# An attention loop one stage shorter, with its causal mask added by TensorE

## What is computed

```python
s_cmp = einsum(q, kc) * scale;  p_cmp = masked_softmax(s_cmp, ends <= t);  o_cmp = p_cmp @ vc
s     = einsum(q, ks) * scale;  p     = masked_softmax(s, kpos <= tq);     o_s   = p @ vs
s     = einsum(q, kw) * scale;  p     = masked_softmax(s, mw);             o_w   = p @ vw
o = g[..., 0:1] * o_cmp + g[..., 1:2] * o_s + g[..., 2:3] * o_w
```

## Time and profile before

| | |
|---|---|
| median of 3 executions | 2720.64 us (2716.98 to 2725.18) |
| the profiled execution | 2725.98 us |
| its span | 2724.3 us |
| busy share TensorE / VectorE / ScalarE | 98% / 68% / 51% |
| attention loop | about 1702 to 1826 us of the span |
| mean granted TensorE clock, whole span | 0.981 |

### The profile page before, as it was taken

The page is one execution under the profiler, slowest core; times in us unless marked ns, Lnnn a source line. Parts: engine busy times, 40 slices in busy tenths (PEclk is TensorE's granted clock), DMA queues, the critical chain, the costliest instruction groups (busy, mean ns, idle before and its releaser), DMA issues.

```text
span 2724.3 us, 42687 instructions
## 1 busy us (share of the span) xinstructions
PE 2658.9 (98%) x16032; PEld 2340.0 (86%) x16032; DVE 1855.1 (68%) x2662; ACT 1400.2 (51%) x1882; POOL 147.9 (5%) x149
## 2 busy tenths in 40 slices
PE   7999999999999999999999999889999999999998
PEld 7999898888888888888888888678888888888887
DVE  4699866677766775677755767756677757765775
ACT  5588755356634553454444544643456535543553
POOL 0001100210000000003100000002200000000003
PEclk9999999999999999999998999789999999999999
DMA  6454335555555555555755665005555555555544
GB/s 210 160 180 146 109 122 168 183 192 185 187 194 190 185 186 192 192 178 174 212 157 171 185 189 171 9 14 185 189 185 188 191 192 186 185 189 193 188 162 147
DMA packets 238535, 464.49 MB, mean 170 GB/s; under 512 B 12506, under 2 KB 14170, under 8 KB 238426
## 3 DMA queue, kind: packets, MB, share of 16 engines
q1 hardware_dynamic: 236922, 460.73, 51.0%
q10 hardware_dynamic: 1504, 2.29, 0.3%
HBM read 460.90 MB, written 2.10 MB: 170 GB/s over the span
## 4 chain that ended last, share of the span: by engine, by line
PE 88%; DVE 4%; DMA 4%; ACT 3%; issue 1%; SPq 0%; DVEq 0%; ACTq 0%
PE bank L1723 47%; PE bank L1726 23%; PE bank L1969 4%; PE bank L1970 4%; PE bank L1971 4%; DVE weight_tail L1083 1%; ACT weight_head L605 1%; PE bank L2005 1%; DMA weight_raw<-in_ffn_w_up 1%; PE bank L2047 1%; DMA w<-in_nsa_cmp_w 1%; DMA weight_raw<-in_cd_w_in 1%; DMA weight_raw<-in_ffn_w_down 1%; ACT prob L1047 1%; PE bank L2084 1%
## 5 line engine op out<-in xcount | busy, mean ns | idle before, releaser
L1083 DVE TENSOR_TENSOR weight_tail<-weight_raw,weight_head 128x2048 fp32r<-128x2048 f32 (+1 forms) x456 | 1000.5, 2195 | 757.2 <-ACT weight_head L605 755.6
L605 ACT ACTIVATE weight_head<-weight_raw 128x2048 fp32r<-128x2048 f32 (+1 forms) x456 | 832.3, 1826 | 969.0 <-DMA weight_raw<-in_ffn_w_up 315.9
L1723 PE MATMUL bank<-norm_in,weight_head 128*128 128x512 f32 x3840 | 1210.8, 397 | 11.4 <-DVE residual L1439 6.7
L1726 PEld LDWEIGHTS bank<-norm_in,weight_tail 128*128 128x128 f32 x3840 | 723.4, 188 | 171.4
L1726 PE MATMUL bank<-norm_in,weight_tail 128*128 128x256 f32 x3840 | 755.9, 278 | 0.0
L1723 PE MATMUL bank<-mixed,weight_head 128*128 128x512 f32 x2176 | 703.6, 398 | 6.7 <-DVE mixed L1500 3.6
L1723 PEld LDWEIGHTS bank<-norm_in,weight_head 128*128 128x128 f32 x3840 | 586.5, 189 | 13.2 <-DVE weight_tail L1083 7.5
L1726 PEld LDWEIGHTS bank<-mixed,weight_tail 128*128 128x128 f32 x2176 | 411.5, 189 | 80.8
L1726 PE MATMUL bank<-mixed,weight_tail 128*128 128x256 f32 x2176 | 463.6, 280 | 0.0
L1723 PEld LDWEIGHTS bank<-mixed,weight_head 128*128 128x128 f32 x2176 | 348.5, 190 | 26.8 <-DVE residual L1439 5.2
L1969 PE MATMUL bank<-norm_in,weight_head 128*128 128x256 f32 x896 | 260.8, 291 | 6.7 <-ACT zx L855 4.4
(11 more groups left out here) (288 smaller groups left out, 1583.1 us busy)
## 6 DMA issues: line engine op xcount, KB each, us to landing
weight_raw<-in_ffn_w_up SPq DMA_DIRECT2D x176, 1024.0 KB, 4.9
weight_raw<-in_ffn_w_down SPq DMA_DIRECT2D x64, 1024.0 KB, 5.0
weight_raw<-in_cd_w_in SPq DMA_DIRECT2D x64, 1024.0 KB, 5.7
weight_raw<-in_ab_w_in SPq DMA_DIRECT2D x56, 1024.0 KB, 4.9
weight_raw<-in_ab_w_out SPq DMA_DIRECT2D x32, 768.0 KB, 4.3
weight_raw<-in_ffn_w_down SPq DMA_DIRECT2D x32, 768.0 KB, 4.2
weight_raw<-in_cd_w_out SPq DMA_DIRECT2D x32, 768.0 KB, 4.2
x_stage<-in_x SPq DMA_DIRECT2D x4, 512.0 KB, 6.0
```

The source lines that it names most:

```text
L605: act.activation(WHEAD[:, off % RING, 0:kt * CW], WRAW[:, off % RING, 0:kt * CW], ACT.Copy)\
L1083: dve.tensor_tensor(WTAIL[:, off % RING, 0:kt * CW], WRAW[:, off % RING, 0:kt * CW], WHEAD[:, off % RING, 0:kt * CW].bitcast(F32), ALU.sub ...
L1723: pe.matmul(bank[c][:, :], head, rhs[:, u * s.kt + k, :], start=u == 0 and k == 0, stop=False)
L1726: mm = pe.matmul(bank[c][:, 0:SEQ], tail, rhs[:, u * s.kt + k, 0:SEQ], start=False, stop=u == s.units - 1 and k == s.kt - 1)
```

## The change

Transposes, value products and the copies that belong to them come one iteration sooner on every engine: TensorE transposes item n - 2 and multiplies item n - 3 in iteration n, ScalarE copies item n - 2, and the output copies of a head (1052 and 1685) stand at even n from 6 on in place of odd n from 7 on. PROB has 3 buffers and another place. Each engine's loop runs one iteration less.

The causal mask is no longer added by VectorE. GpSimd writes a mask of one 128x128 block and a copy of the identity, both in the rounded type fp32r. TensorE accumulates identity times mask onto the last 128 columns of both branches, right behind the scores. VectorE takes the maxima straight from PSUM, and ScalarE reads the scores from PSUM in its exponentials; only the compressed scores still pass through PROB. So the scores of item n now also wait for the exponentials of item n - 2 (p_ready), and for the transposed copy of item n - 3 in place of n - 4. The diff, cut:

```diff
-PROBS = 4
-        MASK = at("causal", places["tri"], [P, 2 * P], F32)
+        IDENT_R = at("ident_r", places["tri"], [P, P], F32R)
+        MASK_R = at("causal", places["ust"], [P, P], F32R)
-        PROB = at("prob", places["norm_in"] + 22528, [P, PROBS, 528], F32)
+        PROB = at("prob", places["norm_in"] + 8192, [P, 3, 528], F32)
...
-            link(pool.memset(MASK[:, :], 0.0))
-            pool.affine_select(out=MASK[:, P:2 * P], in_=MASK[:, P:2 * P], compare_op=ALU.is_ge, fill=NEG,
+            pool.tensor_copy(IDENT_R[:, :], IDENT[:, :]).then_inc(mask_ready, 1)
+            link(pool.memset(MASK_R[:, :].bitcast(F32), 0.0))
+            pool.affine_select(out=MASK_R[:, :], in_=MASK_R[:, :].bitcast(F32), compare_op=ALU.is_ge, fill=NEG,
                                base=0, pattern=[[-1, P]], channel_multiplier=1).then_inc(mask_ready, 1)
...
-            for n in range(last + 6):
+            for n in range(last + 5):
-                if 3 <= n < last + 3:
-                    m = n - 3
+                if 2 <= n < last + 2:
+                    m = n - 2
...
-                    act.activation(PTC[0:NCMP, m % 2, :], bank[2 + m % 2][0:NCMP, P:2 * P], ACT.Copy).then_inc(pt_read, 1)
+                    act.activation(PTC[0:NCMP, m % 2, :], bank[3 - m % 2][0:NCMP, P:2 * P], ACT.Copy).then_inc(pt_read, 1)
...
-                    for r, probs in enumerate((PROB[:, p3, 512:512 + NCMP], PROB[:, p3, 0:nk], PROB[:, p3, SEQ:SEQ + nk])):
-                        act.activation(probs, probs, ACT.Exp, bias=MX[:, 4 * b + r:4 * b + r + 1], scale=SCALE,
+                    if n >= 3:
+                        act.wait_ge(pt_done, n - 2)
+                    branches = ((PROB[:, p3, 512:512 + NCMP], PROB[:, p3, 512:512 + NCMP]),
+                                (PROB[:, p3, 0:nk], bank[b][:, 0:nk]),
+                                (PROB[:, p3, SEQ:SEQ + nk], bank[b][:, SEQ:SEQ + nk]))
+                    for r, (probs, scores) in enumerate(branches):
+                        act.activation(probs, scores, ACT.Exp, bias=MX[:, 4 * b + r:4 * b + r + 1], scale=SCALE,
                                        accum_out=SUMS[:, 4 * b + r:4 * b + r + 1]).then_inc(p_ready, 1)
-                if n >= 7 and n % NT == 1:
+                if n >= 6 and n % NT == 0:
...
-                    if n >= PROBS:
-                        dve.wait_ge(pt_done, n - PROBS + 1)
+                    if n >= 3:
+                        dve.wait_ge(pt_done, n - 2)
                     dve.wait_ge(s_done, n + 1)
-                    dve.tensor_tensor(p3[:, 512:512 + NCMP], bank[2 + b][:, 0:NCMP], CMPM[:, t, :], ALU.add)
-                    dve.tensor_tensor(branches(p3[:, 0:512], nk), branches(bank[b][:, :], nk),
-                                      MASK[:, 2 * P - nk:2 * P].unsqueeze(1).to_broadcast([P, 2, nk]), ALU.add)\
-                       .then_inc(s_read, 1)
+                    dve.tensor_tensor(p3[:, 512:512 + NCMP], bank[2 + b][:, 0:NCMP], CMPM[:, t, :], ALU.add).then_inc(s_read, 1)
+                    dve.tensor_reduce(MX[:, 4 * b + 1:4 * b + 3], branches(bank[b][:, :], nk), AXX, ALU.max)
                     dve.wait_ge(s_read, n + 1)
-                    dve.tensor_reduce(MX[:, 4 * b:4 * b + 1], p3[:, 512:512 + NCMP], AXX, ALU.max)
-                    link(dve.tensor_reduce(MX[:, 4 * b + 1:4 * b + 3], branches(p3[:, 0:512], nk), AXX, ALU.max))
+                    link(dve.tensor_reduce(MX[:, 4 * b:4 * b + 1], p3[:, 512:512 + NCMP], AXX, ALU.max))
...
+                    if n == 0:
+                        pe.wait_ge(mask_ready, 2)
                     if n >= 2:
                         pe.wait_ge(s_read, n - 1)
-                    if n >= 4:
-                        pe.wait_ge(pt_read, 2 * (n - 3))
+                        pe.wait_ge(p_ready, 3 * (n - 1))
+                    if n >= 3:
+                        pe.wait_ge(pt_read, 2 * (n - 2))
...
+                    nk = P * (t + 1)
+                    scores = bank[b][:, :].rearrange("p (r k) -> p r k", r=2)
+                    pe.matmul(scores[:, :, 0:nk], qh, BC[:, 2 * g:2 * g + 2, 0:nk], start=True, stop=False)
+                    pe.matmul(scores[:, :, nk - P:nk], IDENT_R[:, :], MASK_R[:, :].unsqueeze(1).to_broadcast([P, 2, P]),
+                              start=False, stop=True)
                     pe.matmul(bank[2 + b][:, 0:NCMP], qh, KCR[:, g * NCMP:(g + 1) * NCMP], start=True, stop=True)\
                       .then_inc(s_done, 1)
-                if 3 <= n < items + 3:
+                if 2 <= n < items + 2:
...
-                    m = n - 3
+                    m = n - 2
                     b, t = m % 2, m % NT
                     pe.wait_ge(pn_ready, 3 * (m + 1))
-                    pe.wait_ge(s_read, min(m + 3, items))
+                    pe.wait_ge(s_read, min(m + 2, items))
...
-                if n >= 4:
...
-                    m = n - 4
+                if n >= 3:
...
+                    m = n - 3
```

More of the change, by code:

```diff
@@ L1041, in _ @@
                     act.activation(PT[:, m % 2, 0:blocks * P], bank[4 + m % 2][:, 0:blocks * P], ACT.Copy).then_inc(pt_read, 1)
-                    act.activation(PTC[0:NCMP, m % 2, :], bank[2 + m % 2][0:NCMP, P:2 * P], ACT.Copy).then_inc(pt_read, 1)
+                    act.activation(PTC[0:NCMP, m % 2, :], bank[3 - m % 2][0:NCMP, P:2 * P], ACT.Copy).then_inc(pt_read, 1)
                 if n < last:
-                    b, p3, nk = n % 2, n % PROBS, P * (n % NT + 1)
+                    b, p3, nk = n % 2, n % 3, P * (n % NT + 1)
                     act.wait_ge(mx_ready, n + 1)
-                    for r, probs in enumerate((PROB[:, p3, 512:512 + NCMP], PROB[:, p3, 0:nk], PROB[:, p3, SEQ:SEQ + nk])):
-                        act.activation(probs, probs, ACT.Exp, bias=MX[:, 4 * b + r:4 * b + r + 1], scale=SCALE,
+                    if n >= 3:
[5 more added lines that the diff above has]
+                        act.activation(probs, scores, ACT.Exp, bias=MX[:, 4 * b + r:4 * b + r + 1], scale=SCALE,
                                        accum_out=SUMS[:, 4 * b + r:4 * b + r + 1]).then_inc(p_ready, 1)
-                if n >= 7 and n % NT == 1:
+                if n >= 6 and n % NT == 0:
                     h = n // NT - 3
@@ L1633, in _ @@
             dve.wait_ge(gates_ready, 1)
-            dve.wait_ge(mask_ready, 1)
             items = NSA_HEADS * NT
@@ L1639, in branches @@
                 return a.rearrange("p (r k) -> p r k", r=2)[:, :, 0:nk]
-            for n in range(items + 6):
+            for n in range(items + 5):
                 if n in (6, 10):
@@ L1647, in _ @@
                     nk = P * (t + 1)
[L1648 to L1650 removed]
+                    p3 = PROB[:, n % 3, :]
+                    if n >= 3:
+                        dve.wait_ge(pt_done, n - 2)
                     dve.wait_ge(s_done, n + 1)
[L1652 to L1655 removed]
+                    dve.tensor_tensor(p3[:, 512:512 + NCMP], bank[2 + b][:, 0:NCMP], CMPM[:, t, :], ALU.add).then_inc(s_read, 1)
+                    dve.tensor_reduce(MX[:, 4 * b + 1:4 * b + 3], branches(bank[b][:, :], nk), AXX, ALU.max)
                     dve.wait_ge(s_read, n + 1)
[L1657 to L1658 removed]
+                    link(dve.tensor_reduce(MX[:, 4 * b:4 * b + 1], p3[:, 512:512 + NCMP], AXX, ALU.max))
                     dve.tensor_scalar(MX[:, 4 * b:4 * b + 3], MX[:, 4 * b:4 * b + 3], -SCALE, -NEG * 1e-6,
@@ L1673, in _ @@
                     for r in range(2):
-                        pr = PROB[:, m % PROBS, r * SEQ:r * SEQ + nk]
+                        pr = PROB[:, m % 3, r * SEQ:r * SEQ + nk]
                         dve.tensor_scalar(pr, pr, FAC[:, 4 * b + 1 + r:4 * b + 2 + r], None, ALU.mult).then_inc(pn_ready, 1)
-                    pr = PROB[:, m % PROBS, 512:512 + NCMP]
+                    pr = PROB[:, m % 3, 512:512 + NCMP]
                     dve.scalar_tensor_tensor(out=pr, in0=pr, scalar=FAC[:, 4 * b:4 * b + 1], in1=CMP1[:, t, :],
@@ L2035, in _ @@
             items = NSA_HEADS * NT
-            for n in range(items + 4):
+            for n in range(items + 3):
                 if n < items:
@@ L2067, in _ @@
                             pe.transpose(bank[4 + b][:, i * P:(i + 1) * P],
-                                         PROB[:, m % PROBS, r * SEQ + kb * P:r * SEQ + (kb + 1) * P], IDENT[:, :])
+                                         PROB[:, m % 3, r * SEQ + kb * P:r * SEQ + (kb + 1) * P], IDENT[:, :])
                             i += 1
-                    pe.transpose(bank[2 + b][0:NCMP, P:2 * P], PROB[:, m % PROBS, 512:512 + NCMP], IDENT[:, :])\
-                      .then_inc(pt_done, 1)
-                if n >= 4:
-                    m = n - 4
+                    pe.transpose(bank[3 - b][0:NCMP, P:2 * P], PROB[:, m % 3, 512:512 + NCMP], IDENT[:, :]).then_inc(pt_done, 1)
+                if n >= 3:
+                    m = n - 3
                     b, (h, t) = m % 2, divmod(m, NT)
```

## The result

The changed kernel takes 2696.06 us (median of 5 executions, 2693.48 to 2706.1), the kernel before in the same comparison 2716.98 us (5 executions, 2709.49 to 2725.18): ratio 0.9932, 95% interval 0.9911 to 0.9953.

What follows compares the result with a forecast made beforehand. It took a ring of waits and a clock partly at 1.2 GHz to bound the attention loop. Middle 10.9, start -1.5 and end +2 gave 11.4 us gain: 2709 us against the 2720.64 median, range 2699 to 2719.

Steps and rivals of the forecast that it cites:

- step (b): Attention loop: odd scores, VectorE, even normalisation, transposes, odd value product, next odd scores bind at 5.70 us per head.
- part 1: Mask in PSUM: VectorE's start to scaling falls from 1.60 to 1.01 us; each mask product adds 0.12 us on TensorE.
- (e): Attention loop, iterations 6 and 10: VectorE's weight splits sit in front of the new ring, costing 1 us hidden before.
- The clock in the middle: Middle 13 heads: gain 5.9 us if the clock is low as long as before, 15.8 if it stays up; 10.9 taken.
- Rival 2: Attention loop: the clock stays up after the start; gain 15.8 + 0.5 us, time 2704 us; chance 0.17.
- (f): Loop's end, last scores to next projection: one iteration less gains 2 us, between 0 and 3.
- (d): Loop's start: scores wait for exponentials two items back and the copy three back; loss 1.5 us, between 0 and 3.5.
- The sum: Attention loop: middle 10.9, start -1.5 and end +2 make a gain of 11.4 us.
- the one set for being wrong: Whole kernel: a fall of over 20 us would mean the clock, not the ring, was the prize.
- TensorE's wait at the even transposes: Attention loop: TensorE's idle time would stand there, waiting for the normalisation, not at the even value product; no size given.
- rival 4: Middle of the attention loop: the clock settles low, kernel slower; break-even at 43 us low, 2728 us at 60; chance 0.09.

Runs made afterwards that it cites:

- e4: The changed kernel with VectorE taking the maximum of each odd item once more, into unused columns; ratio to the kernel before 0.9958.
- e1: The changed kernel with the mask back on VectorE as an addition and exponentials from PROB, so only the shorter pipeline; ratio to the kernel before 0.9953.
- e3: The changed kernel without the mask product, which leaves out the causal mask inside the last block; ratio to the kernel before 0.9917.
- e6: The kernel before, with TensorE making the four transposes of each odd item twice; ratio to the kernel before 0.9979.
- e8: The changed kernel with the maximum of each odd item taken three more times; 2740.96 us, ratio to the kernel before 1.0068.
- e2: The kernel before with only the mask product, maxima and exponentials from PSUM, at the old pipeline depth; ratio to the kernel before 0.9924.
- e5: The changed kernel with the maximum of each odd item taken two more times; ratio to the kernel before 1.0004.
- e10: e8 with nine useless identity transposes per head in TensorE's idle piece; 2726.8 us, ratio to the kernel before 1.0015.

## Why the prediction was wrong

- **The ring of step (b): right.** It is the one that binds; 5.49 us for the forecast 5.70. The scores took 1.48 (forecast 1.49) and the normalisation 1.21 as forecast; VectorE's part 0.96 for 1.09, and the step from VectorE to TensorE 0.06 for 0.15. Most of the former is the pitch: I took the mask addition's 0.71, and the maximum's is 0.60 (e4). Why the step was shorter is not shown. Over 13 heads 2.7 us. From 6.45 to 5.49 us a head the ring gave 12.5 us. Without part 1 the same sum gave 6.10, and e1 took 6.09.
- **Part 1: right.** The mask product costs 0.12 us in the ring (e3). VectorE's busy time in the loop fell from 89 to 73 us (forecast 17 less). The maximum from PSUM takes 680 ns, that from SBUF took 676, so the forecast's row was right to count the source at nothing. By the two fixed costs in the errata section of "VectorE: DVE Perf Modes" in the Trainium skill, an estimate of the difference is 65 ns; the measured 4 ns do not agree with it.
- **(e) too small:** two heads took 6.29 us behind the weight splits, 1.6 us in all for the forecast 1.0.
- **The clock in the middle: the term that failed.** "So I take the middle" put 7.0 us of low clock into the new middle; there was none. Rival 2 (clock up after the start, chance 0.17) was the case that came. My doubt came from one row, 12.8 us of busy TensorE at 1.2 GHz. But what a busy TensorE does once the clock is low says nothing of how often it falls, and the runs show that in the middle this hangs on the idle time: no fall in e1 with 0.74 us a head, none in e6 with 0.70, six in e8 with up to 1.70. The new ring has no idle piece at all in a steady head.
- **The end, (f): mis-sized.** Forecast +2, it was +7.4. I priced the work left out at the clock that ruled there, and did not ask whether that clock would rule: the mean clock of the end went from 0.61 to 1.00. Why it held is only in part known. With the deep pipeline it fell behind waits for the output copy (1.14 and 0.85 us before, 1.00 in e2); with the shallow one, which has no such wait, it stayed at 1.00 although TensorE idles 0.88 us there (1.61 in e1). But in e5 and e8 it fell at the end with the shallow pipeline too, behind pieces of 2.08 and 2.68 us, and no run changes the end alone.
- **The start, (d): the size right,** -2.0 for -1.5, the reason in part: the scores of item 2 wait 5.17 us for the exponentials. But e1, which has no such wait, has a start of 17.2 us all the same: there TensorE waits 5.53 us at the transposes of item 0, which now stand ahead of the scores of item 3. Each half of the change alone makes the start longer (15.4 us before, 17.2 in e1, 16.8 in e2).
- **The sum** of these: ring 2.7, clock 7.0, splits -0.6 make the middle's 9.1 above the forecast 10.9; end 5.4, start -0.5. 11.4 + 9.1 + 5.4 - 0.5 = 25.4 in the profiled loop, of which the medians show 20.9. My sum also took the clock's cost from a profiled execution with more low clock than most (0.981). Rival 2's 2704 is 8 us above the result, since it held only the middle's clock, with the old ring sum and the end at +2.
- Some luck lies in the range. The forecast started from 2720.64 us, the median of 3 executions, and the kernel before took 2716.98 in the comparison; the ratio 0.9932 on 2720.64 gives 2702, inside 2699 to 2719. The gain was too small by either count (11.4 for 18 to 21).
- Of the signs, the one set for being wrong came by the medians: over 20 us. Its reading, that then the clock and not the ring was the prize, holds by half: in the middle the ring gave 12.5 us and the clock 9.0, and the rest is the end. TensorE's wait at the even transposes, also a sign, was not there.
- The break-even of rival 4 (clock low for 43 us) was never near.

What stays open: why e5's clock fell early and then held with idle pieces of 1.10 us, when that of the kernel before kept falling with 1.13, and why single pieces of 1.48 and 1.61 us left it at 1.00. Where a fall comes within a run of equal heads is not explained by anything here.

## What to carry to other kernels

In a loop in which TensorE waits a little in every turn, work out two things: the ring, from the rows, and TensorE's idle time in a turn of it. If the change takes that away, put the clock that was lost in the steady part into the sum in full, not by half: here it came back whole in the middle in e1, e2, e6 and the change. Treat the loop's ends by themselves: the start was still at 0.80 in the changed kernel, and the end at 0.69 in e2 and 0.88 in e6. Where the ring cannot be shortened, a few useless transposes in the idle piece may pay: 5.5 us here, for four that shorten it by 0.43 us a head. And look at the clock of several executions before taking its cost from one profile.

## What I had not expected of the hardware

- Useless work made two kernels faster (e6 by 0.21%, e10 against e8 by 14.2 of 2741 us), because at 1.2 GHz TensorE's work takes 1.8 times as long (a head 9.51 us at the low clock, 5.32 busy at the high one).
- Each half of the change alone wins back the middle's low clock (9 us in the profile before), so that 15.8 and 17.2 us gave 25.4 together and not 33.
- Exponentials read from PSUM are shorter than from SBUF by 41 ns (451 and 492 ns for 256 columns) and 38 ns (348 and 386 ns for 128). Groups by line, first of the changed kernel, then of the one before:

```profile
L1053 ACT ACTIVATE prob<-bank,small 128x256 f32<-128x256 f32 x32 | 14.4, 451 | 0.0
...
L1053 ACT ACTIVATE prob<-bank,small 128x128 f32<-128x128 f32 x32 | 11.1, 348 | 0.0
...
L1658 DVE TENSOR_REDUCE small<-bank 128x2 f32<-128x512 f32 x16 | 10.9, 680 | 0.0
```

```profile
L1047 ACT ACTIVATE prob<-prob,small 128x256 f32<-128x256 f32 x32 | 15.7, 492 | 0.0
...
L1047 ACT ACTIVATE prob<-prob,small 128x128 f32<-128x128 f32 x32 | 12.3, 386 | 0.0
```

The errata section of "VectorE: DVE Perf Modes" in the Trainium skill gives ScalarE a fixed cost of 172 cycles for a PSUM source and 224 for SBUF, by its 1.2 GHz an estimate of 43 ns. On ScalarE the rows agree within 5 ns (41 and 38), on VectorE they do not (680 from PSUM, 676 from SBUF).
